# Start of a two-layer transformer kernel: the latent tokens loaded amid the first modulation tiles, which are split ten to TensorE and six to VectorE

## The reference

```python
mod   = silu(c)     @ w_ada + b_ada      # 9 * 1024 values, for the latents
mod_c = silu(c_ctx) @ w_ada + b_ada      # the same for the context
s1, sc1, g1, s2, sc2, g2, s3, sc3, g3 = split(mod, 9)
h = h + 0.5 * g1 * swiglu(modulate(rms_norm(h, g_ffn1), s1, sc1), w1_gate, w1_up, w1_down)
h = h + g2 * mixer(modulate(rms_norm(h, g_mix), s2, sc2))       # attention and a Fourier mix
h = h + 0.5 * g3 * swiglu(modulate(rms_norm(h, g_ffn2), s3, sc3), w2_gate, w2_up, w2_down)
# rms_norm(x, g) = x * rsqrt(mean(x*x) + 1e-6) * g ;  modulate(x, s, sc) = x * (1 + sc) + s
```

## Time and profile before

| what | value |
|---|---|
| median of 3 runs | 2606.88 us (2605.81 to 2607.53) |
| the profiled execution, its time | 2612.69 us |
| its span, first to last instruction | 2610.9 us |
| busy, share of the span | PE 97%, DVE 75%, ACT 44%, POOL 30% |
| mean granted TensorE clock | 0.991 of full speed |

### The profile page before, as it was taken

One profiled execution on the slowest core, in us unless ns is written; L12 is line 12 of the kernel. 1 busy time (PEld: TensorE's weight loads), 2 busy tenths in 40 slices (PEclk: granted clock), 3 DMA queues, 4 the chain that ended last, 5 costly groups with the idle time before them and its releaser, 6 DMA issues.

```text
span 2610.9 us, 40249 instructions
## 1 busy us (share of the span) xinstructions
PE 2523.0 (97%) x14986; PEld 2316.8 (89%) x14986; DVE 1945.2 (75%) x3213; ACT 1150.6 (44%) x2131; POOL 786.8 (30%) x614
## 2 busy tenths in 40 slices
PE   7999999999988999999999999999999999899998
PEld 4999999988877899999998999999987787899997
DVE  5888788766498488888756888887567596877776
ACT  5533433443476362433344624333444474544443
POOL 1222121224177231222122312221223285333332
PEclk8999999999999999999999999999999999999999
DMA  6344445214430124444312244443123331133332
GB/s 243 100 147 139 130 129 158 74 59 150 107 90 1 57 85 137 130 134 145 113 61 77 77 148 127 125 146 113 61 65 134 98 78 45 62 96 98 101 104 83
DMA packets 132002, 276.17 MB, mean 106 GB/s; under 512 B 15584, under 2 KB 35296, under 8 KB 130528
## 3 DMA queue, kind: packets, MB, share of 16 engines
q1 hardware_dynamic: 131808, 273.60, 34.1%
HBM read 260.43 MB, written 13.11 MB: 105 GB/s over the span
## 4 chain that ended last, share of the span: by engine, by line
PE 78%; DVE 12%; issue 4%; ACT 3%; DMA 1%; SPq 1%; POOL 0%; ACTq 0%; DVEq 0%; POOLq 0%
PE ring L1841 37%; PE ring L1943 21%; PE ring L1954 14%; DVE wlo L1437 2%; DVE ptl L1261 1%; DVE neg_max L1238 1%; PE row L1777 1%; PE row L1762 1%; ACT pth L1100 1%; PE ring L1797 1%; DVE xl L1548 1%; ACT whi L948 1%; DVE tl L1347 1%; DVE t_lat L1541 1%; DVE prob L1251 1%
## 5 line engine op out<-in xcount | busy, mean ns | idle before, releaser
L1437 DVE TENSOR_TENSOR wlo<-raw,whi 128x512 fp32r<-128x512 f32 (+2 forms) x672 | 508.7, 767 | 280.0 <-ACT whi L948 279.4
L948 ACT ACTIVATE whi<-raw 128x512 fp32r<-128x512 f32 (+2 forms) x672 | 399.1, 605 | 385.7 <-PE ring L1943 240.7
L1841 PE MATMUL ring<-xh,whi 128*128 128x384 f32 (+1 forms) x1280 | 411.8, 322 | 0.6 <-DVE rstd L1416 0.5
L1841 PE MATMUL ring<-xl,whi 128*128 128x384 f32 (+1 forms) x1280 | 411.4, 321 | 0.0
L1841 PE MATMUL ring<-xh,wlo 128*128 128x384 f32 (+1 forms) x1280 | 411.2, 321 | 0.0
L1841 PE MATMUL ring<-th,whi 128*128 128x384 f32 (+1 forms) x960 | 313.6, 327 | 14.3 <-DVE acc L1302 8.2
L1841 PE MATMUL ring<-th,wlo 128*128 128x384 f32 (+1 forms) x960 | 312.1, 325 | 0.0
L1841 PE MATMUL ring<-tl,whi 128*128 128x384 f32 (+1 forms) x960 | 311.9, 325 | 0.0
L636 POOL TENSOR_TENSOR raw<-raw,s_two 128x512 f32<-128x512 f32 x80 | 116.1, 1452 | 619.1 <-DVE wlo L1437 582.4
L1444 DVE SCALAR_TENSOR_TENSOR ada_junk<-ada_tile,row 128x1024 bf16<-128x1024 f32 x256 | 301.3, 1213 | 0.0
L622 POOL TENSOR_TENSOR s_one<-raw 128x512 f32<-128x512 f32 x80 | 105.5, 1319 | 553.6 <-DMA raw<-w_gu 414.5
(11 more groups left out here) (218 smaller groups left out, 5499.1 us busy)
## 6 DMA issues: line engine op xcount, KB each, us to landing
raw<-w_gu SPq DMA_DIRECT2D x352, 256.0 KB, 3.1
ada_tile<-w_turned SPq DMA_DIRECT2D x130, 512.0 KB, 3.7
raw<-w_down SPq DMA_DIRECT2D x96, 256.0 KB, 3.6
raw<-w_down SPq DMA_DIRECT2D x64, 192.0 KB, 2.6
raw<-w_in SPq DMA_DIRECT2D x48, 256.0 KB, 3.4
raw<-w_down SPq DMA_DIRECT2D x64, 128.0 KB, 2.1
raw<-w_out SPq DMA_DIRECT2D x32, 256.0 KB, 8.0
ada_first<-w_first SPq DMA_DIRECT2D x4, 1536.0 KB, 13.3
```

The lines of the kernel that those rows point to most:

```text
L948: act.activation(weights(q, 0, cols)[0], src[:, 0:cols], ACT.Copy).then_inc(whi_ready, 1)
L1437: dve.tensor_tensor(w_l, src[:, 0:cols], w_h.bitcast(F32), ALU.subtract).then_inc(wlo_ready, 1)
L1841: last = pe.matmul(out, w, x, start=(start and k == 0 and m == 0), stop=(k == HALF - 1 and m == 2), skip_group_check=not start)
```

## The change

- TensorE makes tiles 0 to 9 in five units of 256 columns, VectorE tiles 10 to 15. The units are taken in the order 4, 0, 1, 2, 3.
- On SP's queue the four loads of the latent tokens move up, behind the third unit and the second of VectorE's tiles. The load of `bias_ada` moves from the second place to behind them, with a semaphore of its own. The loads of the small constants (`gain` and others) move to behind the last tile.
- ScalarE's third `read_row` stands amid the squares (behind d = 2); the root of the latents is taken at once after the squares, and the last two `read_row` behind it.
- VectorE adds the squares up after two of its six tiles, makes a third tile, inverts and widens the root (`widen_first`), and makes the other three tiles then.
- TensorE makes three units, sums over the partitions, makes the fourth, spreads the root, makes the fifth.
- `split_hi` and `split_lo` of the first two weight pieces move into `norm`, behind the last `read_row` on ScalarE and behind the scales on VectorE.
- The eight squares of the context, which stood in one block behind the root, are spread two at a time behind `xh` of d = 1 to 4 in the loop of the norm.

```diff
-ADA_COLS = 384
-FIRST_UNITS = 4
-UC = ADA_COLS // P
+FIRST_UNITS = 5
+UC = 2
+UNIT_ORDER = (4, 0, 1, 2, 3)
@@ SyncE
-            load_first(0)
+            load_first(UNIT_ORDER[0])
             sp.dma_start(cond_row[:], c_rows).then_inc(rows_loaded, 16)
+            load_first(UNIT_ORDER[1])
             load_ada(FIRST_TILES)
-            load_first(1)
+            load_first(UNIT_ORDER[2])
             load_ada(FIRST_TILES + 1)
+            for i in range(HALF):
+                load_x(i)
+            sp.dma_start(bias_ada[:], b_ada).then_inc(bias_loaded, 16)
+            load_first(UNIT_ORDER[3])
+            load_early(FIRST_TILES + 2)
+            load_early(FIRST_TILES + 3)
+            load_first(UNIT_ORDER[4])
+            load_early(FIRST_TILES + 4)
+            load_early(FIRST_TILES + 5)
             for dst, src in ((gain, gains), (gain_final, g_final), ...):
                 sp.dma_start(dst[:], src).then_inc(more_loaded, 16)
-            load_first(2)
-            load_early(FIRST_TILES + 2)
-            load_first(3)
-            load_early(FIRST_TILES + 3)
-            for i in range(HALF):
-                sp.dma_start(h[:, 2 * i:2 * i + 2, 0:SEQ], x_t[...]).then_inc(x_loaded[i], 16)
             load_w(0, 2)
             sp.dma_start(h[:, :, SEQ:TOK], ctx_t).then_inc(ctx_loaded, 16)
@@ ScalarE, norm
-                std(n, width, 0)
                 if n == 0:
-                    act.wait_ge(ctx_loaded, 16)
-                    for d in range(KD):
-                        square_ctx(d)
+                    split_hi(0, 2)
+                else:
+                    std(n, width, 0)
...
                         act.activation(xh[:, d, a:b], t1, ACT.Identity, ...)
+                        if n == 0 and p == 0 and 1 <= d <= HALF:
+                            if d == 1:
+                                act.wait_ge(ctx_loaded, 16)
+                            square_ctx(2 * d - 2)
+                            square_ctx(2 * d - 1)
@@ ScalarE, start
             read_row(0)
             read_row(1)
-            read_row(2)
             for d in range(KD):
...
-                if d == HALF + 1:
-                    read_row(3)
-            split_hi(0, 2)
+                if d == 2:
+                    read_row(2)
+            std(0, TOK, 0)
+            read_row(3)
+            read_row(4)
@@ VectorE, start
             for i in range(FIRST_TILES, FIRST_TILES + 2):
                 ada_columns(...)
-            for i in range(FIRST_TILES + 2, FIRST_TILES + EARLY):
-                ada_columns(...)
-            ada_bias(FIRST_TILES, FIRST_TILES + EARLY)
             for d in range(KD - 1):
                 sum_first(d)
+            early_columns(FIRST_TILES + 2)
+            widen_first(0, TOK)
+            for i in range(FIRST_TILES + 3, FIRST_TILES + EARLY):
+                early_columns(i)
+            ada_bias(FIRST_TILES, FIRST_TILES + EARLY)
             dve.wait_ge(more_loaded, 16 * 5)
             dve.wait_ge(first_turned, FIRST_UNITS)
-            for c in range(2):
-                dve.tensor_tensor(modv[:, c, 0:FIRST_UNITS * UC], ...)
-            split_lo(0, 2)
+            dve.tensor_tensor(modv[:, :, 0:FIRST_TILES], ...)      # both vectors in one
             norm(0, TOK, 0, 0)                                     # split_lo(0, 2) now in it
@@ TensorE, start
-            for u in range(FIRST_UNITS):
-                ... unit u, then turn_first(u - 1)
-            turn_first(FIRST_UNITS - 1)
-            sum_chunks(0, TOK, 0)
-            spread_rstd(0, TOK, 0)
+            first_unit(0)
+            first_unit(1)
+            turn_first(0)
+            first_unit(2)
+            turn_first(1)
+            sum_chunks(0, TOK, 0)
+            turn_first(2)
+            first_unit(3)
+            spread_rstd(0, TOK, 0)
+            first_unit(4)
+            turn_first(3)
+            turn_first(4)
```

More of the change, by code:

```diff
@@ L285, in build @@
         assert room >= 92160, room
-        ada_first = [sb(f"ada_first{i}", [P, KD, ADA_COLS], F32, work + 12288 * i) for i in range(4)]
-        ada_early = sb("ada_early", [P, 2, D_MODEL], F32, work + 49152)
+        ada_first = [sb(f"ada_first{i}", [P, KD, UC * P], F32, work + 8192 * i) for i in range(FIRST_UNITS)]
+        ada_early = sb("ada_early", [P, 4, D_MODEL], F32, work + 40960)
         sq_lat = sb("sq_lat", [P, 2, SEQ], F32, work + 57344)
         ada_junk_first = sb("ada_junk_first", [P, 2, D_MODEL], BF16, work + 61440)
+        ada_rows = sb("ada_rows", [2, 2, UC * P], F32, work + 83968)
         ada_junk = sb("ada_junk", [P, 2, D_MODEL], BF16, work + 75776)
-        ada_rows = sb("ada_rows", [2, 2, ADA_COLS], F32, work + 83968)
         sq_ctx = sb("sq_ctx", [P, KD, CTX], F32, work)
@@ L341, in build @@
         cond_ready, qkg_ready = sem("cond_ready"), sem("qkg_ready")
-        ada_first_loaded = [sem(f"ada_first_loaded{i}") for i in range(4)]
+        ada_first_loaded = [sem(f"ada_first_loaded{i}") for i in range(FIRST_UNITS)]
         ada_loaded = [sem("ada_loaded_even"), sem("ada_loaded_odd")]
-        early_loaded = [sem("early_loaded_even"), sem("early_loaded_odd")]
+        early_loaded = [sem(f"early_loaded{i}") for i in range(4)]
+        bias_loaded = sem("bias_loaded")
         rows_loaded, rows_ready = sem("rows_loaded"), sem("rows_ready")
@@ L479, in _ @@
             sp.dma_start(cond[:], c_cols).then_inc(const_loaded, 16)
-            sp.dma_start(bias_ada[:], b_ada).then_inc(const_loaded, 16)
             def source(kind, *at):
@@ L1038, in _ @@
             act.preload_act_table(ACT.Silu)
-            act.wait_ge(const_loaded, 16 * 2)
+            act.wait_ge(const_loaded, 16)
             act.activation(scond[:], cond[:], ACT.Silu).then_inc(cond_ready, 1)
@@ L1043, in _, with read_row @@
             act.preload_act_table(ACT.Sqrt)
[L1044 to L1049, removed]
+            def read_row(j):
+                act.wait_ge(ada_row_mm, j + 1)
+                if j >= 2:
+                    act.wait_ge(first_turned, j - 1)
+                act.activation(ada_rows[:, j % 2], ring[0][0:2, j % 2 * SEQ:j % 2 * SEQ + UC * P], ACT.Copy).then_inc(ada_row_read, 1)
             read_row(0)
             read_row(1)
-            read_row(2)
             for d in range(KD):
@@ L1489, in invert, with widen_first @@
                 dve.reciprocal(rms_inv[:, a // P:b // P], rms[:, a // P:b // P]).then_inc(inv_done, 1)
+            def widen_first(n, width):
+                invert(n, width, 0)
+                dve.wait_ge(inv_done, 2 * n + 1)
+                for m in range(halves(width)[0][1] // P):
+                    last = dve.tensor_scalar(rstd[:, m * P:(m + 1) * P], ones[:], rms_inv[:, m:m + 1], None, ALU.mult)
+                last.then_inc(rwide[0], 1)
             def norm(n, width, layer, stage, before=None):
@@ L1495, in norm @@
                     col = MODC * layer + 3 * KD * stage
-                    dve.wait_ge(first_ready, 2)
+                    dve.wait_ge(first_ready, 1)
                     ready = [i for key, i in plan.ada.items() if key[0] < n]
@@ L1511, in norm @@
                         split_lo(stages[n]["first"], 2)
[L1512 to L1517, removed]
                 if before is not None:
+                    widen_first(n, width)
                     late_residual(before, late.pop(0))
+                else:
+                    split_lo(0, 2)
                 if layer is None:
@@ L1583, in sum_first, with early_columns @@
                     dve.tensor_tensor(acc[:, 0:SEQ], acc[:, 0:SEQ], sq_lat[:, d % 2], ALU.add).then_inc(acc_first[0], 1)
-            dve.wait_ge(const_loaded, 16 * 2)
-            dve.wait_ge(cond_ready, 1)
+            def early_columns(i):
+                dve.wait_ge(early_loaded[i - FIRST_TILES - 2], 16)
+                ada_columns(i, ada_early[:, i - FIRST_TILES - 2], cond_row, ada_junk_first)
             dve.wait_ge(rows_ready, 1)
```

40 lines of the change are left out of this document (22 added, 18 removed).

## The result

| | before | changed |
|---|---|---|
| median of 22 runs each | 2608.74 us (2603.64 to 2613.83) | 2612.10 us (2609.23 to 2614.65) |
| the profiled execution | 2612.69 us | 2613.98 us |
| its span | 2610.9 us | 2612.2 us |

The ratio of the changed kernel to the one before is 1.0012, 95% interval 1.0006 to 1.0017: about 3 us slower. The prediction had it 0.95 us slower, 3.3 us at the end of its range; the measured 2612.10 lies outside the range (2603.9 to 2610.2), and by the ratio the loss is three times the forecast. (The kernel before also had a median 1.9 us higher over 22 runs than over the three that the forecast started from.) The wait for GpSimd and the half clock behind it came where the prediction put them, both larger; another 2.0 us went at a place where it had seen no loss, TensorE's fourth unit.

What follows compares the result with a forecast made beforehand. It took the way to the first product, up to ScalarE's silu of the first gate, as the bound: -3.0 (start) + 2.6 (GpSimd wait) + 1.65 (half clock) - 0.3 (slack) = +0.95 us, median 2607.8 us, range 2603.9 to 2610.2.

Steps and rivals of the forecast that it cites:

- The wait for GpSimd: TensorE, before the context's sums: they start 9.3 us behind the first t1 instead of 6.7, costing 2.6 us.
- the half clock behind it: TensorE behind the context's sums: half clock for some 3.4 us from 48.0, costing 1.65 us.
- start of the loop: First t1 in the norm's loop: starts at 38.7 us instead of 41.70, a gain of 3.0 us.
- TensorE beside it: TensorE's units, sums and spread beside VectorE's tiles: a unit takes 3.55 us, reading and turning end at 36.6.
- no bound yet: Before the first t1: TensorE's rows are ready 0.1 us ahead of VectorE, so they do not delay it.
- What the moved squares cost: Context's squares in the norm's loop: TensorE's context sums wait for GpSimd's adds, eating 2.6 of the 3.0 us.
- The clock: TensorE from 48.0 us: half clock for some 3.4 us costs 1.65 us, bounds 0 to 5 us.
- slack of the silu: ScalarE's silu of the first gate came 0.3 us after TensorE's gate before; this slack takes 0.3 us off.
- the shift at the silu is the shift at the end: Behind the first gate's silu the program is unchanged, so its shift, +0.95 us, carries to the kernel's end.
- the clock holds over the gap: Rival, at TensorE's gap before the context's sums: no half clock, silu 0.7 us earlier than before, 2606.2 us; chance 0.18.
- Late transfers: Rival, loads at the start: tile 12 lands 2.5 us later and all else follows, +3.4 us, 2610.3 us; chance 0.13.
- the gain carries through: Rival, context's sums ready in time: the whole -3.0 us stays, 2603.9 us; chance 0.12 with what lies towards 2606.2.

Runs made afterwards that it cites:

- thin adds: Changed kernel with GpSimd's five further adds of the context's squares over 16 columns instead of 256; 2609.66 us, one run.
- squares early: Changed kernel with four context squares ahead of the norm's loop, the other four behind xh of d = 1 and 2; 2608.19 us, ratio 0.9998 to before.
- every gap filled: Changed kernel with context's squares and first two weight-piece splits early, unused matmuls in TensorE's gaps; 2607.37 us, ratio 0.9994 to before.

## Why the prediction was wrong

**Most of the path was right, its sizes were not.** It was worked out as start of the loop, wait for GpSimd, half clock, silu, and the profile shows these; but the start was bound by TensorE's fifth unit and not by VectorE's tiles. In the prediction's sum the silu was 0.95 late; it was 4.65.

**The step that failed first: "TensorE beside it".** It priced the fourth unit at 3.55 us, at the full clock, on the ground that a unit's records took 0.33 us for 384 columns. The unit took 6.42, the fifth then ended at 38.1 instead of 35.8, and the wait of VectorE that the text called "no bound yet" was 2.71 us. The rows to see it were there: the sums of before ran at half clock behind waits of only 1.48 and 0.97 us (34.93, shown above), and the same five idle microseconds that I had written down ahead of the sums (three units end near 19, sums start at 24.1) are a longer gap than the 1.89 us that I used for the clock 20 us further on. I drew on that row for one gap and not for the other. Cost: 40.66 instead of 38.7, 2.0 us. The run with that gap filled gives the 38.4, so the half clock is what cost them. That the five idle microseconds alone brought it is not shown: part of it came in two kernels with the gap filled.

**"What the moved squares cost".** Direction and mechanism were right; the run with only this part moved (1.0016), and the one with it taken back (0.9998), show that the squares are the loss. The size was short by 1.0 us: I let VectorE keep its pace of before while GpSimd's adds now ran beside its rests. Two rests took 2.35 us and not 1.28, t1 of d = 4 came 7.7 behind the first t1 and not 6.4, the squares behind it late by as much, and the sums 10.3 and not 9.3 behind it. The thin adds show it (6.6 and 8.8).

**"The clock".** The half clock behind the gap was forecast for 3.4 us and lasted over 6 us. (Half of 3.4 is 1.7, not the 1.65 of the sum; that changes nothing.) From the sums to the first matmul of the context's columns it took 13.0 us, against 10.6 before and 10.2 with the gap filled: 2.4 us or 2.8, not 1.65. With the slack of the silu, from the sums to the silu it took 17.5 us instead of 15.5: 2.05, where the prediction had 1.35, another 0.7.

The misses are 2.0, 1.0 and 0.7, together the 3.7 between 0.95 and 4.65.

**That the shift at the silu is the shift at the end** held roughly: 4.65 at the silu and 3.4 in the medians, 4.1 and 4.2 (median 2612.01 against 2607.8) with the squares moved in the kernel before. 0.6 of the shift went in TensorE's next wait, which was shorter; a stretch of half clock that comes or goes explains more in a single pair of profiles.

**The rivals.** That the clock holds over the gap was wrong here (0.50 behind 3.50 us), and it would have been at the forecast size: with the thin adds it fell to 0.50 behind 2.12 us. So the rule that the prediction takes from the Trainium skill, "TensorE: Matmul & The Clock Gate", section "HAM oscillation — how this bites in real kernels", which would keep the clock over so short a gap, does not hold in this kernel. Late transfers were not the cause: tile 12 was taken up at 25.70 us, forecast 25.8. That the gain carries through did not hold in any run.

**What stays open.** With the squares early the start is up to 3.8 us earlier than before and the silu 1.2 at most. The rows of one such kernel account for the difference, but no run took its two causes, the rests beside GpSimd's adds and the half clock behind the sums, apart. Why the half clock comes there is not known: even with every gap filled it was 1.00 from 36 to 47 us and 0.81 behind. And the 41.70 and 63.86 of before are of one execution, 4 us over its median; by the 0.8 us that the clock over the sums made in another execution, gains read against them may be that much too large. What the ratio shows is that the rest of the change, the units and the order of loads, is worth nothing measurable (0.9998), and not the 3 us of its start.

## What to carry to other kernels

Work moved off a block into the gaps of a paced loop costs nothing on its engine, yet its result comes at the loop's pace: look who adds it up, who waits for the sum, and what is queued behind that wait. Price a stretch of TensorE at half clock as well, wherever it stood idle or was thinly filled ahead of it, before it is called hidden (here half clock followed idle times from 5 us down to less than 1). And time two engines that will now run side by side by rows in which they did.

## What the runs showed of the hardware

- From 23.7 to 33.9 us TensorE was busy 98% and more, and the granted clock was still 0.50 over the sums over partitions (one moving column a matmul) and 0.55 over the fourth unit. With the 5 us ahead filled it stayed at 1.00 over the sums in four kernels, and over the fourth unit in two of them.
- One set of instructions meets half clock at different places in different executions of nearly the same program: the fourth unit took 6.42, 5.94, 6.23, 5.32, 5.05 and 5.26 us in six executions of five kernels in which nothing ahead of it on TensorE differs.
- Half clock followed a wait of TensorE of 1.89 us (kernel before, 85.70) and one of 2.12 us (thin adds); with waits of 0.43 and 0.82 us in a row (squares early) it came too.
- A VectorE instruction with two SBUF inputs that started while GpSimd was adding two tiles in SBUF took 1.23 instead of 0.74 us, a pair of them 2.35 instead of 1.28; where the GpSimd add started second, the VectorE instruction took 0.75 and the add 1.24 instead of 0.73. VectorE's widening of the root, which reads one tile, was slowed as well (1.38 instead of 0.87 us for four); an instruction with an input in PSUM was not.
